# Head 0's loads under the last value chunk, the first sample's products on GpSimd, and the attention heads written out

## The reference

```python
z = rmsnorm(x) @ w_in                      # q | k | v | forget logit | rnn x | rnn gate
# prompt: 8 heads of width 64, causal, with a forget bias
s = q @ k.T * ATT_SCALE + cq[:, None] - ck[None, :]      # c = cumsum(log f)
A = softmax(where(kpos <= qpos, s, -inf)) @ v
# sample n: 4096 cached tokens in 32 pages of 128, found by page_table[n]
k_past = cache_k[page_table[n]]; v_past = cache_v[page_table[n]]; f_past = cache_logf[page_table[n]]
c = cumsum(concat(f_past, f_new))
A_n = softmax(q_n @ concat(k_past, k_n).T * ATT_SCALE + c_n - c) @ concat(v_past, v_n)
x = x + concat(rmsnorm(A), rmsnorm(R)) @ w_out           # R: recurrent branch
x = x + ConvGLU_FFN(rmsnorm(x))
```

## Time and profile before

| what | value |
|---|---|
| median of 3 runs | 3229.03 us (3224.3 to 3231.68) |
| the profiled execution, its own time | 3231.55 us |
| its span, first to last instruction | 3229.8 us |
| PE busy | 2987.9 us, 93% |
| DVE / ACT / POOL busy | 1427.4 / 755.3 / 1205.8 us |
| stage 2, last product of L2224 to last chain step of attention | about 612 to 1450 us |
| mean granted PE clock | 0.951 of full speed |

### The profile page before, as it was taken

How to read it: one execution, slowest core, us unless ns; L and a number is a source line. 1 busy time by engine, 2 the same in 40 slices (tenths; PEclk the granted TensorE clock), 3 DMA queues, 4 the chain that set the end, 5 groups by cost and what they waited for, 6 DMA issues and landing times.

```text
span 3229.8 us, 46435 instructions
## 1 busy us (share of the span) xinstructions
PE 2987.9 (93%) x15701; PEld 2606.4 (81%) x15701; DVE 1427.4 (44%) x1921; ACT 755.3 (23%) x1533; POOL 1205.8 (37%) x577
## 2 busy tenths in 40 slices
PE   4999999777798989988999999999999998999998
PEld 4899999643454545547999999999999998999998
DVE  5312444377665666615135444554455543212221
ACT  7000333322232323334011000000000003443442
POOL 1111111137765666605773222222222223454443
PEclk9999999877888989998999999999999999999999
DMA  7212332447776787544451111111111114555553
GB/s 224 74 66 91 108 114 100 117 112 244 239 224 206 231 259 237 186 128 162 136 184 60 45 43 52 52 41 45 46 52 46 47 53 167 197 181 175 186 196 108
DMA packets 249057, 422.72 MB, mean 131 GB/s; under 512 B 44693, under 2 KB 152418, under 8 KB 244370
## 3 DMA queue, kind: packets, MB, share of 16 engines
q1 hardware_dynamic: 167986, 322.58, 31.6%
q10 hardware_dynamic: 80616, 97.07, 9.0%
q0 software_dynamic: 288, 1.05, 0.1%
HBM read 337.21 MB, written 83.46 MB: 130 GB/s over the span
## 4 chain that ended last, share of the span: by engine, by line
PE 75%; SPq 5%; DVE 5%; issue 4%; DMA 4%; POOL 3%; ACT 3%; ACTq 0%; DVEq 0%; POOLq 0%
PE PS L2559 34%; PE PS L2224 14%; PE PS L2647 4%; PE PS L2649 4%; PE PS L2443 4%; PE PS L2648 4%; SPq L603 3%; SPq L596 2%; PE PS L2467 1%; DMA Vpg<-in_cache_v 1%; PE PS L2427 1%; PE PS L2352 1%; PE PS L2429 1%; DVE YT L2173 1%; DVE MP L1825 1%
## 5 line engine op out<-in xcount | busy, mean ns | idle before, releaser
L2559 PE MATMUL PS<-MH,VS 128*128 128x416 f32 (+1 forms) x4000 | 1080.4, 351 | 3.8 <-issue 2.2
L2559 PEld LDWEIGHTS PS<-MH,VS 128*128 128x128 f32 x4000 | 749.4, 188 | 14.1 <-issue 5.5
L2559 PE MATMUL PS<-ML,VS 128*128 128x416 f32 (+1 forms) x2000 | 699.8, 350 | 0.0
L2559 PEld LDWEIGHTS PS<-ML,VS 128*128 128x128 f32 x2000 | 376.0, 188 | 2.6 <-issue 0.8
L1071 POOL TENSOR_TENSOR DL<-DR,DH 128x1408 fp32r<-128x1408 f32 x80 | 258.5, 3231 | 286.3 <-ACT DH L1496 286.2
L924 POOL TENSOR_TENSOR prod<-Kpg,qb 128x1024 f32<-128x1024 f32 x118 | 279.4, 2367 | 167.5 <-DMA Kpg<-in_cache_k 81.1
L2443 PE MATMUL PS<-PT,VA 128*65 128x416 f32 (+16 forms) x816 | 335.2, 495 | 2.4 <-ACT PT L1359 1.8
L2647 PE MATMUL PS<-GH,DH 128*128 128x416 f32 (+1 forms) x880 | 315.0, 358 | 17.1 <-DVE GL L2155 8.9
L1000 POOL CAST VS<-VR 128x1024 fp32r<-128x1024 f32 x52 | 62.9, 1209 | 689.2 <-PE PS L2559 687.6
L2649 PE MATMUL PS<-GH,DL 128*128 128x416 f32 (+1 forms) x880 | 310.8, 353 | 0.0
L2648 PE MATMUL PS<-GL,DH 128*128 128x416 f32 (+1 forms) x880 | 309.2, 351 | 0.0
(11 more groups left out here) (286 smaller groups left out, 4313.4 us busy)
## 6 DMA issues: line engine op xcount, KB each, us to landing
Kpg<-in_cache_k SPq DMA_DIRECT2D x256, 256.0 KB, 4.6
Vpg<-in_cache_v SPq DMA_DIRECT2D x256, 256.0 KB, 4.2
DR<-in_w_down SPq DMA_DIRECT2D x80, 704.0 KB, 4.1
gT<-GO ACTq DMA_DIRECT2D x110, 208.0 KB, 1.9
VR<-in_w_up SPq DMA_DIRECT2D x44, 512.0 KB, 3.3
GRb<-gT SPq DMA_DIRECT2D x31, 416.0 KB, 5.0
WR<-in_w_stream SPq DMA_DIRECT2D x21, 512.0 KB, 3.4
GRa<-gT SPq DMA_DIRECT2D x24, 416.0 KB, 5.6
```

The costliest lines, as they stand in the source:

```text
L2559: mm = e.matmul(PS[:, j, 0:full(j)], w[:, u, k], x[:, k, j * BW:j * BW + full(j)], start=(k == 0 and q == 0), stop=(k == KC - 1 and q == 2))
```

## The change

1. **Head 0's rows.** `Qst`, `Kst2`, `rden`, `cb`, `knb` are placed on tiles of stage 1 that die early. SP issues the loads of `Qst` after the last scan (`r_sc`), of `Kst2` after the last product of the recurrent branch (`r_y`), both while PE is in its last value chunk, and the load of the decay rows into `rden` after POOL has set it to 1, which waits for the last store from `RX` (`r_st`). POOL then sets `QA` without waiting for the loads.
2. **Cached logarithms.** `ctot` moves to `Vpg`, `cwith` into `cb` itself, `lpage` and the sums to `AO`, `xtp` to `VA`. `Kpg` and `prod` are free, and the key pages of sample 0 are loaded right after the page numbers.
3. **Sample 0.** All 16 products are POOL's. DVE takes the first four scores between pieces 32, 36, 40 and 43 of head 0 (`EARLY`) and the other twelve at tiles 5 to 16.
4. **Heads 1 to 6 are written out** on all engines: Python loops take the place of `Fori`.

```diff
+EARLY = (32, 36, 40, 43)
...
-            plan[4 + g].append(("products", g))
-            plan[5 + g].append(("scores", g))
+            if g >= len(EARLY):
+                plan[g + 1].append(("scores", g))
...
-        ctot = Kpg[:, 0:2].rearrange("p a b n -> p (a b n)")
-        cwith = Kpg[:, 2:4].rearrange("p a b n -> p (a b n)")
-        lpage = prod[:, 0:2].rearrange("p a b n -> p a (b n)")
+        ctot = Vpg[:, 2:4].rearrange("p a b n -> p (a b n)")
+        cwith = cb[:].rearrange("p s h -> p h s")
+        lpage = AO[:, 1, 0:NPG * NH].rearrange("p (g n) -> p g n", g=2)
...
-            e.wait_ge(g_mm, 5 * NIN)
             for st in z_st:
                 e.wait_ge(st, 128 + 32 + 1)
             e.wait_ge(f_st, 80)
-            e.wait_ge(c_att2, 2)
-            fetch_head(0)
+            e.wait_ge(r_sc, 4)
+            e.dma_start(Qst[0:HD], qT[0:HD, :]).then_inc(st_ld, 16)
+            e.dma_start(Qst[HD:P], qT[0:HD, :]).then_inc(st_ld, 16)
+            e.wait_ge(r_y, 5)
+            e.dma_start(Kst2[0:HD], kT[0:HD, :]).then_inc(st_ld, 16)
+            e.dma_start(Kst2[HD:P], kT[0:HD, :]).then_inc(st_ld, 16)
+            e.wait_ge(c_att2, 1)
+            e.dma_start(rden[HD + 2:HD + 4], decayT[:, 0, :]).then_inc(x_first, 16)
             e.wait_ge(phase_end, 4)
...
+            def fetch_first_keys(g):
+
+                if g >= 4:
+                    e.wait_ge(kpp, g - 3)
+                fetch_pages("cache_k", Kpg, kg_ld, 0, g)
+
+            for g in range(4):
+                fetch_first_keys(g)
             e.wait_ge(c_att, 1)
             fetch_values(0, 0)
-            fetch_query(0, 0)
             e.sem_inc(vd, 3)
+            for g in range(4, 8):
+                fetch_first_keys(g)
             e.wait_ge(prep, 7)
             e.wait_ge(dec, 2)
             fetch_head(1)
-            e.wait_ge(pg_ld, 32)
+            for g in range(8, PAGES // 2):
+                fetch_first_keys(g)
...
-            with e.Fori(0, 2) as ii:
+            for ii in range(2):
                 for v in range(2):
                     sync_head(2 * ii + 1 + v, 1 - v, load_order(False, False), 2)
...
+            pool_products(0, 0, 0, 4)
+            e.wait_ge(kpp, 4)
             e.wait_ge(lf_pg, 32)
             prepare(0, 0, 3, 7)
             e.wait_ge(prep, 7)
-            e.wait_ge(c_att2, 4)
+            pool_products(0, 0, 4, 8)
+            e.wait_ge(kpp, 8)
+            prepare(1, 1, 0, 3)
+            e.wait_ge(prep, 10)
+            pool_products(0, 0, 8, 16)
...
             for p in range(len(PIECES)):
                 piece_max(0, p, (2, 3))
-            e.wait_ge(phase_end, 4)
+                if p in EARLY:
+                    if p == EARLY[0]:
+                        e.wait_ge(phase_end, 4)
+                    page_scores(0, 0, EARLY.index(p))
```

More of the change, by code:

```diff
@@ L36 @@
 NREAL = 2072
+KEEP = 368
 NHN = 3
@@ L303, in build @@
         AO = sb("AO", [P, 2, TP], F32, m2)
-        rden = sb("rden", [P, TP], F32, m2)
         RD = sb("RD", [HD, 2, DEN_W], F32, m2)
@@ L890, in prepare @@
                 if first == 0:
-                    e.wait_ge(st_ld, 80 * i + 80)
+                    e.wait_ge(st_ld, 80 * i + 64)
                 for n in range(first, last):
-                    if not (isinstance(i, int) and i == 0 and n == 0):
-                        e.wait_ge(prep, own + n)
+                    e.wait_ge(prep, own + n)
                     e.sem_inc(go, 1)
@@ L914, in pool_products @@
                 for g in range(first, last):
-                    done = 16 * s - DVE_FIRST + g
+                    done = 16 * s + g
                     e.wait_ge(kg_ld[g % 4], 32 * (4 * s + g // 4) + 32)
                     e.wait_ge(nw_ld, 32 * s + 32)
-                    e.wait_ge(kd, 16 * s + g - 3)
-                    if g == 0:
+                    if done > 3:
+                        e.wait_ge(kd, done - 3)
+                    if g == 0 and s:
                         e.wait_ge(kf, 4 * s - 2)
-                    if not (isinstance(s, int) and s == 0 and g == DVE_FIRST):
+                    if done:
                         e.wait_ge(kpp, done)
@@ L1379, in _ @@
             act_head(0, 0, PLANS[0])
-            with e.Fori(0, 3) as ii:
+            for ii in range(3):
                 for v in range(2):
@@ L1949, in dve_head @@
                             piece_max(i + 1, n, (2, 3, 6))
-                        if what == "products":
-                            if n < DVE_FIRST:
-                                page_products(0, 0, n)
                         if what == "scores":
```

114 lines of the change are left out of this document (53 added, 61 removed).

## The result

The changed kernel takes 3197.26 us (median of 4 runs, 3188.13 to 3199.22) beside 3226.66 us for the kernel before on the same chip: ratio 0.9902, 95% interval 0.9878 to 0.9926, so 29 us less by the medians. In a second series it took 3193.18 us (4 runs) beside 3228.43: 0.9883 [0.9851, 0.9914], 35 us less. The prediction was 3195, 34 us less. The profiled execution took 3197.86 us; its span is 33.7 us shorter than that of the earlier trace rows.

A forecast was written before the change was run, and what follows sets the result against it. PE held 75% of the chain, nearly all loss lying in head 0 and its lead-in. 18 us there plus 16 from heads 1 to 6 off 3231.55 gave 3197.5, from the median 3195; own range 3184 to 3206, full 3173 to 3214.

The forecast's parts named there:

- Step 1: Start of head 0, 612.4 to 635 us: big loads leave the chain, PE starts near 625; gain 10, bounds 6 and 12.
- Step 2: Head 0's pieces, before 635 to 677 us: four scores added, two hidden in DVE's waits, two paid; 3 us lost.
- Step 3: Running sums, before 678 to 691.4 us: DVE pays for meeting POOL's instructions; 4 us lost, between 0 and 6.
- Step 4: Tiles 5 to 20, before 690 to 742.1 us: end near 724; 15 us here, running gain 18, bounds 10 and 26.
- Step 5: Head 0 from "end", 742.1 to 832.9 us: the 18 us pass undiminished; 0 more, bounds −5 and +5.
- Step 6: Heads 1 to 6: PE's two branch stalls, 9.65 us, and SP's loop work, 6, go; 16 us, bounds 5 and 28.
- SP's share: Heads 1 to 4: the loop's register instructions at SP's page loads cost 1.5 us a head, 6 us.
- rival "more is gained": SP's loop work worth 5 us in each of four heads, and PE's clock rises; 3178 us, chance 0.15.
- "only half": Head 0 gives 8 us and loops 8, or head 0 gives 16 and later heads nothing; 3213 us, chance 0.2.
- rival "slower": Written-out heads are new code whose fetching stalls, 4.8 us a packet on 12 packets; 3253 us, chance 0.06.
- rival "nothing": Head 0's earlier start is waited away at piece 32, products more than 50 us late; 3229 us, chance 0.04.

The follow-up runs named there:

- the second profile: Profile of the changed kernel run again, unchanged, beside the other follow-up kernels: 3193.18 us, 0.9883; heads 1 to 6 in 522.0 us.
- the eight profiles: One profile from each run with heads 1 to 6 written out on all engines; those heads take 521.9 to 529.5 us, mean 525.6.
- experiment 1: Changed kernel with the loops over heads 1 to 6 back on all five engines: 3220.02 us, 0.9965 of the kernel before.
- experiment 4: Kernel before with only heads 1 to 6 written out on all engines: 3209.29 us, 0.9947 of the kernel before.
- Experiments 5: Changed kernel with SP's loads of head 0's rows held back to the end of the projection: 3199.87 us, 0.9889 of the kernel before.
- experiments 6: Changed kernel with the last store from RX issued by SP ahead of the loads of Kst2: 3193.14 us, 0.9872 of the kernel before.
- experiment 8: Changed kernel with the four early scores after pieces 20, 25, 26 and 38: 3185.74 us, 0.9850 of the kernel before.
- experiment 7: Changed kernel with POOL's products 4 to 15 held until DVE's running sums end, head 1's preparation ahead of them: 3203.0 us, 0.9903.
- experiment 2: Changed kernel with the loop over heads 1 to 6 back on PE alone: 3206.91 us, 0.9930 of the kernel before.
- 9: Changed kernel with both the store ahead of Kst2's loads and early scores after pieces 20, 25, 26 and 38: 3187.3 us, 0.9869.

## Why the prediction came out right

The time, 3195 against 3197 and 3193, is right, and so are its two halves: 18 us from head 0 (measured 17.5 to the start of head 1, 15.7 in the second profile) and 16 from heads 1 to 6 (14.8; 18.7 by the mean of the eight profiles). Timed one by one the halves give 11 us (experiment 1, 5 to 17) and 17 us (experiment 4, 8 to 26), so the second is borne out by the time and the first rests on the profiles. Inside head 0 the terms were off by −3.8, −3.4, +1.5, +2.9 and +2.3 us and cancelled: that head 0 came out at 17.5 is luck, in a sum whose steps were in the right order.

- **Step 1, the start: 10 us predicted, 6.2 measured.** The mechanism and its order held. The term that failed is the landing of the store, "4.2 us under way": it took 7.5. The 4.2 was the median over stores that met none of these loads; this one was issued 3.7 to 8 us after four loads of 0.5 MB each, which the change itself has moved there. Experiments 5 (12.1 us with the loads directly ahead) and 6 (the memset 5 us earlier with the store ahead) show it. The step counted what the moved DMAs wait for and not what waits behind them. A second, smaller term: of the copy's 1.24 to 2.84 it took 1.5, and beside POOL's memsets it was 2.79; the decay rows' own way, 3.0 in the sum, took 2.0.
- **Step 2, the pieces: 3 us lost predicted, 6.4 measured.** The products were early, as said (634.5 to 645.5; no score waited for POOL). What failed is "two lie where DVE waits for the cached sums on PE, two are paid". At pieces 32 to 43 next to none is hidden: four scores of 1.2 and L1855's 2.1 make 6.9. Experiment 8 puts all four earlier, three of them ahead of piece 32, and gets 4.8 us back.
- **Step 3, the running sums: 4 us predicted, 2.5 in the sums.** L1855's 2.1, counted under step 2, has the same cause. Experiment 7 shows it: without POOL beside them all durations are those of before. The Trainium skill, "SBUF — State Buffer", section "Who interferes with whom", says that two-input DVE operations and POOL's reads exclude each other. The trace agrees: the scan, the 64-column addition and POOL's cast wait, 1.2, 1.5 and 3.9 us. L1855, with one input, and its 1.48 us beside a memset in experiment 8 are outside that sentence; the runs show them by themselves. The section also says that a DVE reduction never contends, and the scores beside running products take 1.20 to 1.22 us, as in the earlier trace rows.
- **Step 4, tiles 5 to 20: 15 us predicted, 17.9 measured.** POOL was the bound named, and the arithmetic of eight products at 2.65 us holds (699.45 to 720.4), but from 699 and not from 691, because product 8 waits for score 4, which DVE reaches only after the longer sums and tile 5. The term that was too long is the tail: behind the last score four tiles took 6 us and not 10, though the clock was low there:

```profile
721.70:727.70 6.00, 5.38 (x15) 3.70 (x16) 3.36 (x7) 1.43 (x3) 5.41 (x8) 0.54 0.91 295
```

  The 2.5 us for a tile were the pace of the stretch before, in which DVE was busy 44.1 of 52.1 us. PE's work became the 27 us of the step's upper bound, by a clock of 0.96 while POOL's products ran (699.4 to 721.7); that it wasn't the bound there is argued from POOL's products, which stand 0.29 us apart.
- **Step 5: 0 predicted, 0.1 and 2.2 measured.** As said, L1903 stands beside POOL's subtraction again (4.46 us), and SP's issuing is the chain behind.
- **Step 6: 16 us predicted, 14.8 and 22.3 measured in the two profiles.** In time, experiment 4 gives 17 us from the unrolling alone, and the ratio of experiment 1 lies 20 and 26 us above the changed kernel's two. The stalls are gone (no idle time before PE's first product of head 3). The step priced a branch at its stall, 4.8 us; experiment 2 has 13 us for two stalls of 8.6 together, 3.8 of the rest in head 3 with its slow stretch. What speaks for a total near 16 and not above is that another wait takes their place; that is read off the profiles and no run tests it. PE of the changed kernel in head 3, waits by releaser (us in total, times, longest); the second profile and experiment 4 have it too (5.0 and 5.5), and in the kernel before the same head had no wait for value pages:

```profile
PE PS L2480 <- DMA Vpg<-in_cache_v: 5.3, 1, 5.3
PE PS L2365 <- DVE MP L1850: 5.1, 2, 2.8
```

  SP's share, 6 predicted, measures 7 ± 3. The step allowed that position may explain the difference of heads 3 and 5; written out, they take 89.8 and 89.4 us in the mean of the eight profiles, so position alone doesn't.

The rival "more is gained" (3178, a ratio of 0.984) lies outside both intervals, and so does "only half" (3213, 0.995). (The prediction's text calls 3173 the low rival; the rival itself stands at 3178.) The rival "slower" is refuted: there are 74 instruction packets instead of 80, and no stall without a releaser stands at the head starts. The rival "nothing" failed at its own point, since products were 15 us and more ahead of piece 32.

## What to carry to other kernels

- When a load is moved earlier, list what is issued behind it on any queue at that time, stores above all, and price their landing from a row where the queues are as full as they will be; here 4.2 us became 7.5, and 12.1 when the loads were issued just ahead.
- A small vector operation between two large GpSimd ones costs the rest of a GpSimd operation, whatever its size; place it, or the GpSimd work, by that. Still let them overlap when GpSimd's lane is the later bound: 4.6 us paid bought 14.
- Writing heads out can be worth more than the branch stalls that the profile shows (13 us against 8.6, where one profile is good to 3), since the matrix engine comes out of an idle gap at half its clock; other waits do the same, and one moved into the place of the stalls here. And a gain at the start of a chain of engines counts only up to the next lane's bound: tune there (experiment 8) before the start (experiments 6 and 9).
